# Expert selection by sorted maxima, the step's turnings reordered, and first semaphores raised earlier, in a one-core block of two layers

## What is computed

```python
def _hier_moe(h, w_rg, b_rg, w_re, b_re, w_g, w_u, w_d):
    ...
    g_prob = jax.nn.softmax((hf @ w_rg).astype(jnp.float32) + b_rg.astype(jnp.float32), axis=-1)
    g_top, g_idx = lax.top_k(g_prob, 1)
    e_logits = ((hf @ w_re).astype(jnp.float32) + b_re.astype(jnp.float32)).reshape(T, N_GROUPS, EXPERTS_PER_GROUP)
    e_in = jnp.take_along_axis(e_logits, g_idx[:, :, None], axis=1)[:, 0]
    e_top, e_idx = lax.top_k(jax.nn.softmax(e_in, axis=-1), TOP_K)
    wts = g_top * e_top / jnp.sum(e_top, axis=-1, keepdims=True)
    eid = g_idx * EXPERTS_PER_GROUP + e_idx
    ...
    def expert(args):
        xb, e = args
        return (jax.nn.silu(xb @ w_g[e]) * (xb @ w_u[e])) @ w_d[e]
```

## Time and profile before

| what | value |
|---|---|
| median of 3 runs | 701.5 us |
| lowest and highest | 700.43 and 703.64 us |
| the profiled execution | 699.65 us, its span 697.9 us |
| TensorE busy | 644.7 us, 92% |
| VectorE busy | 369.2 us, 53% |
| ScalarE busy | 283.5 us, 41% |
| mean granted clock of TensorE | 0.989 of full speed |
| moved by the transfers | 174.75 MB, mean 250 GB/s |

### The profile page before, as it was taken

One profiled execution on the slowest core, in us unless ns is written; L12 is line 12 of the kernel. 1 busy time (PEld: TensorE's weight loads), 2 busy tenths in 40 slices (PEclk: granted clock), 3 DMA queues, 4 the chain that ended last, 5 costly groups with the idle time before them and its releaser, 6 DMA issues.

```text
span 697.9 us, 11071 instructions
## 1 busy us (share of the span) xinstructions
PE 644.7 (92%) x4357; PEld 482.5 (69%) x4357; DVE 369.2 (53%) x651; ACT 283.5 (41%) x447; POOL 53.9 (8%) x74
## 2 busy tenths in 40 slices
PE   7999999899999999998999999799999986778793
PEld 4999997799999999995797888534444432224363
DVE  6686964777666777675686573621212120103275
ACT  6864463565555555545847621201101100010376
POOL 1000000400000000003185500000000000000000
PEclk9999999999999999999999999999999999899998
DMA  9944541657755555107604169999699999999901
GB/s 326 345 133 159 203 150 46 243 178 239 234 181 180 180 180 180 61 0 256 241 22 171 51 226 428 423 395 434 239 429 430 425 428 426 428 423 428 398 34 60
DMA packets 54488, 174.75 MB, mean 250 GB/s; under 512 B 4662, under 2 KB 29362, under 8 KB 48050
## 3 DMA queue, kind: packets, MB, share of 16 engines
q1 hardware_dynamic: 53776, 172.54, 64.4%
q10 hardware_dynamic: 674, 1.69, 0.6%
HBM read 173.17 MB, written 1.05 MB: 250 GB/s over the span
## 4 chain that ended last, share of the span: by engine, by line
PE 69%; DMA 13%; DVE 10%; ACT 5%; issue 2%; SPq 0%; POOL 0%; DVEq 0%; ACTq 0%; POOLq 0%
PE ps L1742 14%; PE ps L1743 14%; PE ps L1744 14%; DMA arena<-in_w_moe_dram 7%; PE ps L2249 6%; DMA W<-in_w_ple_gate_dram 6%; PE ps L2235 3%; PE ps L2259 3%; PE ps L2284 3%; PE ps L1939 2%; DVE wpg_low L1666 1%; PE ps L2087 1%; DVE arena L1413 1%; PE ps L1714 1%; PE ps L2038 1%
## 5 line engine op out<-in xcount | busy, mean ns | idle before, releaser
L1742 PE MATMUL ps<-hT_high,w_up_high 128*128 128x256 f32 x352 | 99.7, 283 | 1.7 <-DVE w_up_low L1249 1.7
L1744 PE MATMUL ps<-hT_high,w_up_low 128*128 128x256 f32 x352 | 99.6, 283 | 0.0
L1743 PE MATMUL ps<-hT_low,w_up_high 128*128 128x256 f32 x352 | 99.6, 283 | 0.0
L1742 PEld LDWEIGHTS ps<-hT_high,w_up_high 128*128 128x128 f32 x352 | 67.5, 192 | 2.6 <-DVE w_up_low L1249 2.2
L1743 PEld LDWEIGHTS ps<-hT_low,w_up_high 128*128 128x128 f32 x352 | 67.5, 192 | 0.3
L1744 PEld LDWEIGHTS ps<-hT_high,w_up_low 128*128 128x128 f32 x352 | 67.5, 192 | 0.0
L1249 DVE TENSOR_TENSOR w_up_low<-W,w_up_high 128x1024 fp32r<-128x1024 f32 x44 | 53.3, 1239 | 23.9 <-ACT w_up_high L783 23.9
L783 ACT CAST w_up_high<-W 128x1024 fp32r<-128x1024 f32 x44 | 44.6, 1047 | 28.5 <-PE ps L1744 28.5
L942 ACT ACTIVATE arena<-ps 128x256 f32<-128x256 f32 x9 | 3.4, 383 | 117.9 <-PE ps L2249 117.9
L1742 PE MATMUL ps<-h_high,dense_high 128*128 128x256 f32 x160 | 45.7, 286 | 0.0
L1743 PE MATMUL ps<-h_low,dense_high 128*128 128x256 f32 x160 | 45.3, 283 | 0.0
(11 more groups left out here) (471 smaller groups left out, 1364.1 us busy)
## 6 DMA issues: line engine op xcount, KB each, us to landing
W<-in_w_moe_dram SPq DMA_DIRECT2D x25, 2048.0 KB, 19.9
arena<-in_w_moe_dram SPq DMA_DIRECT2D x19, 2048.0 KB, 25.5
W<-in_w_up_dram SPq DMA_DIRECT2D x22, 1024.0 KB, 8.4
W<-in_w_in_dram SPq DMA_DIRECT2D x8, 2048.0 KB, 10.9
W<-in_w_down_dram SPq DMA_DIRECT2D x11, 1024.0 KB, 5.0
hh<-in_w_moe_dram SPq DMA_DIRECT2D x4, 2048.0 KB, 28.7
W<-in_w_out_dram SPq DMA_DIRECT2D x2, 2048.0 KB, 9.0
W<-in_w_o_dram SPq DMA_DIRECT2D x2, 2048.0 KB, 8.4
```

The costliest lines, as they stand in the source:

```text
L1742: pe.matmul(o, lhs[0], rhs[0], start=first, stop=False, skip_group_check=True)
L1743: pe.matmul(o, lhs[0], rhs[1], start=False, stop=False, skip_group_check=True)
L1744: return pe.matmul(o, lhs[1], rhs[0], start=False, stop=last_k, skip_group_check=True)
```

## The change

Five edits, all between the logits and the end of the expert loop:

- The best two experts come from a sorted list: `max` gives the eight largest of a token's 32 masked logits, `max_index` their places, for each token block by itself; a cast and two compares with the column numbers make the two masks. The mask of the other groups is made and applied in one instruction. For the groups the search stays as it was.
- The number of rounds is counted against eight marks, the first of them -1, instead of seven and an added one. The marks are written ahead of the last logits.
- VectorE raises its six first semaphores ahead of the scaling of the logits. TensorE raises its six between 4 and 10 zero products instead of behind its wait for the rounds, and the 19 zero products become 14.
- TensorE scatters one token block at a time and turns the activations between the two; the turning of the one-hots stays behind the second.
- ScalarE copies the activations ahead of the scatter weights.

```diff
@@ -309,11 +309,14 @@
         e32 = [v3(take(64), 2) for _ in range(3)]
         chosen = v3(take(32).bitcast(BF16), 2)
         ranks = e32[0]
-        off[0] += 80
+        top8, at8 = v3(take(16), 2), v3(take(16).bitcast(mybir.dt.uint32), 2)
+        atf = v3(take(4), 2)
+        off[0] += 28
         g4 = [v3(take(8), 2) for _ in range(4)]
         sm = [take(2) for _ in range(12)]
         rcnt = take(8)
-        rgt = take(56)
+        rgt = take(64)
+        marks = take(8)
@@ -940,10 +943,10 @@
 
                 act.wait_ge(sig("upw_used"), n * UPC + 2 * UPC)
                 act.activation(sg, ps[:, 2, 0:F_EXP], ACT.Silu).then_inc(sig("sg_ready"), 1)
+                act.wait_ge(sig("at_done"), n + 2)
+                act.copy(aT, v3(ps[:, 3, 0:256], 2)).then_inc(sig("aT_ready"), 1)
                 act.wait_ge(sig("oht_done"), n + 2)
                 act.copy(SC, ps[:, 0, 0:256]).then_inc(sig("sc_ready"), 1)
-                act.wait_ge(sig("at_done"), n + 2)
-                act.copy(aT, v3(ps[:, 3, 0:256], 2)).then_inc(sig("aT_ready"), 1)
@@ -1543,6 +1546,10 @@
                 dve.tensor_tensor(x_tok[:, b, :], x_tok[:, b, :],
                                   ps[:, 4 + 2 * b:6 + 2 * b, :].rearrange("p a b -> p (a b)"), ALU.add).then_inc(sig("x_ready"), 1)
                 turned(3, "norm_ffn_g_2", (2 * b, 2 * b + 1))
+            for name in ("hot_ready", "oh_ready", "ohw_ready", "xga_ready", "xgb_ready", "a_ready"):
+                dve.sem_inc(sig(name), 1)
+            link(dve.tensor_copy(marks, iot[:, 0:SEQ].rearrange("p (m t) -> p m t", t=CAP)[:, :, 0]))
+            link(dve.tensor_scalar(marks[:, 0:1], ones[:, 0:1], -1.0, None, ALU.mult))
             for b in range(TB):
                 dve.wait_ge(sig("std_ready"), 2 * 3 + b + 1)
                 link(dve.reciprocal(stat[:, 14 + b:15 + b], stat[:, 14 + b:15 + b]))
@@ -1555,42 +1562,41 @@
...
-            def first_max(vals, top, hot, io, n):
-
-                link(dve.tensor_reduce(top, vals, AX, ALU.max))
-                link(dve.tensor_tensor(hot, vals, wide(top, n), ALU.is_equal))
-                link(dve.scalar_tensor_tensor(hot, hot, -64.0, io, ALU.mult, ALU.add))
-                link(dve.tensor_reduce(sm[11], hot, AX, ALU.min))
-                link(dve.tensor_tensor(hot, hot, wide(sm[11], n), ALU.is_equal))
-
-            first_max(gl_, sm[0], g4[0], io4, N_GRP)
+            link(dve.tensor_reduce(sm[0], gl_, AX, ALU.max))
+            link(dve.tensor_tensor(g4[0], gl_, wide(sm[0], N_GRP), ALU.is_equal))
+            link(dve.scalar_tensor_tensor(g4[0], g4[0], -64.0, io4, ALU.mult, ALU.add))
+            link(dve.tensor_reduce(sm[11], g4[0], AX, ALU.min))
+            link(dve.tensor_tensor(g4[2], g4[0], wide(sm[11], N_GRP), ALU.not_equal))
             dve.tensor_tensor(g4[1], gl_, wide(sm[0], N_GRP), ALU.subtract).then_inc(sig("gsub_ready"), 1)
 
-            link(dve.tensor_scalar(g4[2], g4[0], -NEG, NEG, ALU.mult, ALU.add))
             em = e32[0]
-            link(dve.tensor_tensor(em.rearrange("p b (g e) -> p b g e", g=N_GRP),
-                                   el_.rearrange("p b (g e) -> p b g e", g=N_GRP),
-                                   g4[2].unsqueeze(3).broadcast_to([P, 2, N_GRP, EPG]), ALU.add))
-            first_max(em, sm[1], e32[1], io32, N_EXP)
-            link(dve.scalar_tensor_tensor(em, e32[1], 3 * NEG, em, ALU.mult, ALU.add))
-            first_max(em, sm[2], e32[2], io32, N_EXP)
+            link(dve.scalar_tensor_tensor(em.rearrange("p b (g e) -> p b g e", g=N_GRP),
+                                          g4[2].unsqueeze(3).broadcast_to([P, 2, N_GRP, EPG]), NEG,
+                                          el_.rearrange("p b (g e) -> p b g e", g=N_GRP), ALU.mult, ALU.add))
+            for b in range(TB):
+                dve.max(top8[:, b, :], em[:, b, :]).then_inc(sig("top_ready"), 1)
+            for b in range(TB):
+                dve.wait_ge(sig("top_ready"), b + 1)
+                dve.max_index(at8[:, b, :], top8[:, b, :], em[:, b, :]).then_inc(sig("top_found"), 1)
+            dve.wait_ge(sig("top_found"), 2)
+            link(dve.tensor_copy(atf, at8[:, :, 0:2]))
+            for i in range(2):
+                dve.tensor_tensor(e32[1 + i], io32, atf[:, :, i:i + 1].broadcast_to([P, 2, N_EXP]), ALU.is_equal)\
+                   .then_inc(sig("top_marked"), 1)
+            dve.wait_ge(sig("top_marked"), 2)
             dve.tensor_tensor(chosen, e32[1], e32[2], ALU.add).then_inc(sig("sel_ready"), 1)
-            dve.tensor_tensor(sm[4], sm[2], sm[1], ALU.subtract).then_inc(sig("msub_ready"), 1)
+            dve.tensor_tensor(sm[4].unsqueeze(2), top8[:, :, 1:2], top8[:, :, 0:1], ALU.subtract).then_inc(sig("msub_ready"), 1)
             dve.wait_ge(sig("rank_done"), at("rank_done", 1))
             dve.wait_ge(sig("sel_ready"), at("sel_ready", 1))
...
-            marks = iot[:, 0:SEQ].rearrange("p (m t) -> p m t", t=CAP)[:, 1:MAXR, 0]
-            link(dve.tensor_tensor(v3(rgt, 8), rcnt.unsqueeze(2).broadcast_to([P, NGRP8, MAXR - 1]),
-                                   marks.unsqueeze(1).broadcast_to([P, NGRP8, MAXR - 1]), ALU.is_gt))
+            link(dve.tensor_tensor(v3(rgt, 8), rcnt.unsqueeze(2).broadcast_to([P, NGRP8, MAXR]),
+                                   marks.unsqueeze(1).broadcast_to([P, NGRP8, MAXR]), ALU.is_gt))
             link(dve.tensor_reduce(rtab[:, 0:8], v3(rgt, 8), AX, ALU.add))
-            link(dve.tensor_scalar(rtab[:, 0:8], rtab[:, 0:8], 1.0, None, ALU.add))
             link(dve.tensor_tensor_scan(rtab[:, 8:16], ones[:, 0:8], rtab[:, 0:8], 0.0, ALU.mult, ALU.add))
             dve.tensor_copy(rint, rtab).then_inc(sig("rounds_ready"), 1)
             link(dve.scalar_tensor_tensor(ranks, v3(ps[:, 3, 0:64], 2), 1.0, chosen, ALU.add, ALU.mult))
             link(dve.tensor_scalar(RK, ranks, -1.0, None, ALU.add))
-            for name in ("hot_ready", "oh_ready", "ohw_ready", "xga_ready", "xgb_ready", "a_ready"):
-                dve.sem_inc(sig(name), 1)
@@ -2203,7 +2209,10 @@
             turn_x(3, 1)
             logits(1)
             tri, every = counts[:, 0:P], counts[:, P:2 * P]
-            keep_busy(2, 19)
+            keep_busy(2, 4)
+            for name, n in (("gxa_done", 1), ("gxb_done", 1), ("oht_done", 1), ("at_done", 1), ("upw_used", UPC), ("downw_used", DNC)):
+                pe.sem_inc(sig(name), n)
+            keep_busy(2, 10)
             pe.wait_ge(sig("sel_ready"), at("sel_ready", 1))
             pe.matmul(ps[:, 3, 0:32], tri, chosen[:, 0, :], start=True, stop=True)
@@ -2218,8 +2227,6 @@
             keep_busy(2, 3)
             pe.wait_ge(sig("rounds_ready"), 1)
             pe.wait_ge(sig("step_clear"), 2)
-            for name, n in (("gxa_done", 1), ("gxb_done", 1), ("oht_done", 1), ("at_done", 1), ("upw_used", UPC), ("downw_used", DNC)):
-                pe.sem_inc(sig(name), n)
...
-            def scatter(n, signal="scatter_done"):
+            def scatter(n, b, signal="scatter_done"):
 
                 pe.wait_ge(sig("ypa_ready"), n + 1)
                 pe.wait_ge(sig("ypb_ready"), n + 1)
-                for b in range(TB):
-                    for half in range(2):
-                        last = pe.matmul(ps[:, 4 + 2 * b + half, :], SC[:, b * P:(b + 1) * P], Yp[:, half, :],
-                                         start=False, stop=True, skip_group_check=True)
-                    last.then_inc(sig(signal), 1)
+                for half in range(2):
+                    last = pe.matmul(ps[:, 4 + 2 * b + half, :], SC[:, b * P:(b + 1) * P], Yp[:, half, :],
+                                     start=False, stop=True, skip_group_check=True)
+                last.then_inc(sig(signal), 1)
@@ -2289,9 +2295,10 @@
             def pe_step(n, g):
                 gather(n, g)
                 expert_up(n, g)
-                scatter(n)
+                scatter(n, 0)
+                turn_act(n)
+                scatter(n, 1)
                 turn(n)
-                turn_act(n)
                 expert_down(n, g)
@@ -2318,7 +2325,8 @@
                 with pe.Fori(0, rounds) as r:
                     pe_step(begun + r, g)
                 begun = pe.value_load(rint[0:1, 8 + g:9 + g], min_val=1, max_val=NGRP8 * MAXR)
-            scatter(begun, "moe_done")
+            for b in range(TB):
+                scatter(begun, b, "moe_done")
```

## The result

| | before | after |
|---|---|---|
| median of 8 runs each | 702.21 us | 698.03 us |
| lowest and highest | 700.43 and 703.64 us | 695.75 and 700.55 us |
| ratio, with 95% interval | | 0.9941 (0.9926 to 0.9955) |
| the profiled execution, its span | 699.65, 697.9 us | 695.75, 694.0 us |
| mean granted clock | 0.989 | 0.980 |

The change made the kernel 4.2 us, 0.59%, faster (3.2 to 5.2 us by the interval). That is just beyond the 0.5% that a measurement of this kernel can tell. The span of the profiled execution is 3.9 us shorter.

A forecast was written before the change was run, and what follows sets the result against it. Bound by TensorE until the transfers' stop near 491 to 496 us, by weight transfers behind it. Start of the gather 2.4 us plus two steps 1.0 us made 3.4 us, off 701.5: 698.1 us, range 696.5 to 701.0.

The forecast's parts named there:

- count of rounds: On VectorE, counting the rounds loses one linked addition: 0.21 us saved.
- load behind the hole: SyncE's weight load issued at 495.47 us, ending the transfers' stop in the expert stage: claimed 3.4 us sooner.
- The limit: From the load behind the hole on, transfers set the time: the end moves as much as that load, later savings are lost.
- The choice: Choosing experts on VectorE: 14 instructions of 3.51 us become a sorted choice of 1.90 us, saving 1.61 us.
- The slow rival: In the choice on VectorE, new operations cost a scan's 8 ns an element: 1.0 us later, time 699.1 us, chance 0.12.
- The raises: Between rounds and first gather, VectorE's six raises cost 0.60 us, all saved; TensorE's own preparation lay hidden beside VectorE.
- the first case of my two: VectorE's moved raises run while the last product is in the pipe, so the 0.99 us wait for TensorE hides them.
- The bubble: TensorE's raises among the zero products might make the ranks wait 0.2 us; counted as nothing.
- The step: From scatter to first down product, 0.96 us becomes 0.46: 0.50 us saved a step, 1.0 us for two steps.
- The cap: The load behind the hole can come about 6 us sooner before the transfers themselves are the limit.
- The hole left: The transfers' stop in the expert stage was to shorten to about 2.6 us.
- The slower rival, the clock: TensorE's clock falls on the gate products: 7 us at 1.2 GHz cost 3.5 us, 10.5 us give 703.4 us; chance 0.08.

The follow-up runs named there:

- delay_behind: Kernel after with 12 more zero products in each step of groups 2 to 7; ratio to before 0.9937 (0.9916 to 0.9957), 698.23 us.
- delay_ahead: Kernel after with 12 more zero products in each step of groups 0 and 1; ratio to before 1.001 (0.999 to 1.003), 703.05 us.
- sel_only: Kernel before with the sorted choice of experts alone, 19 zero products kept; ratio to before 0.9976 (0.9954 to 0.9997).
- zero19: Kernel after with 4 and 15 zero products instead of 4 and 10; not timed, in its trace the rank products start 3.82 us behind the choice's start instead of 3.19.
- dve_raises: Kernel before with only VectorE's six raises moved ahead; not timed, in its trace the gather starts 2.21 us behind the rounds, as before.
- pe_raises: Kernel before with only TensorE's six raises moved, between 4 and 15 zero products; not timed, in its trace the gather starts 2.20 us behind the rounds.
- skip_if: Kernel after with TensorE jumping over the scatter in the first round of group 0; 696.67 us, ratio to before 0.9914 (0.9894 to 0.9934).
- step_only: Kernel before with the scatter in two parts, activations turned between them and copied first, alone; ratio to before 0.9987 (0.9967 to 1.0006).
- sem_only: Kernel before with both engines' raises moved, TensorE's between 4 and 15 zero products; ratio to before 0.9976 (0.9964 to 0.9988).
- after_again: Kernel after, unchanged, run once more beside skip_if; 697.68 us, ratio to before 0.9934 (0.9916 to 0.9953).

## Why the prediction was right

The forecast was 698.1 us, the median is 698.03. That they agree to 0.1 us is luck: two misses cancel. The forecast took 3.4 us off the median of three runs, 701.5; the median of all eight is 702.21, 0.7 us more, and the change brought 4.2 us, 0.8 more than forecast. Right were the limit and the way from each part to the end; every term was a little small. By steps:

| step | predicted, us | measured, us |
|---|---|---|
| choice, to the end of the sum | 1.61 | 1.74 |
| count of rounds | 0.21 | 0.24 |
| raises, rounds to gather | 0.60 | 0.69 |
| start of the gather | 2.4 | 2.67 |
| two steps | 1.0 | 1.17 |
| load behind the hole | 3.4 | 3.84 |
| landing of the gate weights, on the clock of the trace | 3.4 | 3.93 |

**The limit.** The transfers behind the hole kept their length (121.41 and 120.98 us to the gate load's issue), the stretch behind the last landing too (38.29 us), and what was saved there came to nothing. delay_behind and delay_ahead show both halves.

**The choice.** I took MAX as one pass of 0.192 us started 0.12 us ahead of the next, and that was right: 0.185 us each, and two in 0.29 us. I took MAX_INDEX as two passes of 0.19 us started 0.12 us apart; it is a load of the eight values of 0.07 to 0.09 us, and a search of 0.18 that starts 0.06 to 0.08 us behind the load. Here lie the 0.13 us that the term was small: the second search ended 0.90 us behind the start of the masked addition, where I had 1.03. The slow rival, the scan's price of 8 ns an element, is wrong: 32 elements cost 0.185 us in all. It was one scan of the trace, 4x256 in 2.05 us; two others of the kernel before take 0.68 us for 4x256 and 1.22 us for 128x512, under 3 ns an element, and would have made the rival 0.3 us instead of 1.0. The Trainium skill's "Vector Engine (DVE) Microarchitecture Reference", section 3.9, has the positions found by two instructions; the trace agrees, MATCH_VALUE_LOAD and FIND_INDEX8 stand there as two rows each time. The 1.74 us could all be had only because five zero products went: sel_only and zero19 put that at 0.7 and 0.6 us.

**The raises.** The sum was right within 0.1 us, its reason half wrong. I had booked VectorE's 0.60 us as the path and TensorE's preparation as hidden beside it, "still hidden, barely". That holds without the raises on either side. But in the kernel before, TensorE's six raises, which I priced at VectorE's 0.10 us, cost at least 0.12 to 0.13 each behind its wait for the rounds, and TensorE was as late as VectorE (2.21 us behind the rounds in dve_raises, 2.20 for VectorE in pe_raises). I had named VectorE alone as the path; dve_raises, which moves VectorE's alone, gains nothing at all. A pair of equally late engines looks in the chain of waits like one of them, since the chain names only the last.

VectorE's raises hid where I had put them, the first case of my two: from the turning of the second token block to the next instruction VectorE takes 1.20 us with the six raises between (440.38 to 441.58 us after) and without (440.08 to 441.28 before).

The bubble that I had counted at nothing was nothing: 4.27 us for 19 zero products with and without raises among them. The Trainium skill's "TensorE: Matmul & The Clock Gate", in the section on the array's architectural detail, gives TensorE a queue of 64 instructions, and by that the raises run ahead of the products still queued; the rows agree with it, though no run here varies the depth.

**The step.** Mis-sized by 0.08 us a step. I had 0.50 of the 0.96 us between scatter and down products, it became 0.52; beyond that the down products themselves went from 3.64 to 3.57 us. They start behind a wait for ScalarE before, and no longer do; in skip_if's first step, where they do again, they take 3.64.

**The cap.** "The issue can come about 6 us sooner" was too low, and the reason is a step that failed. I had taken the hole's start, near 489.7 us, as fixed by bytes already under way. By the shares, added up, the transfers stopped near 489.66 us before and 488.78 after, 46.74 and 45.57 us behind the start of the choice: 1.17 us sooner. Two stretches, 456 to 460 us, first of the kernel before, then of after:

```profile
456.00:460.00 4.00, 4.00 (x44) 1.25 (x40) 1.04 (x3) 0.00 (x0) 0.00 (x0) 1.00 0.89 348
```

```profile
456.00:460.00 4.00, 4.00 (x40) 1.04 (x32) 0.00 (x0) 0.00 (x0) 0.00 (x0) 1.00 0.99 422
```

Before, the transfers had a dent here. The first slots of the expert stage came free, and the next load was issued, at 457.48 us before and 455.10 after, and with the earlier issue the dent is gone. That the transfers ran short of work there is a reading, and the other traces bear it out: in step_only, dve_raises and pe_raises the same load is issued 14.5 to 14.6 us behind the start of the choice, as before (14.56), and of the two whole microseconds behind it the lower has 246, 311 and 279 GB/s (197 before); in sel_only and sem_only it is issued at 13.5 and 13.8 us, and the lower has 410 in both. So the cap, counted on the gate load, is about 173.96 - 166.28 = 7.7 us, of which the change takes 4.3. It did not bind here.

**The hole left.** I expected it 3.4 us shorter, 2.6 us long. By the shares that are left unused it went from 6.7 us (489 to 500 us before) to 4.0, 2.7 less. It is the same step: the hole's end moved by 3.84, its start by 1.17 us.

**The slower rival, the clock.** I had put it on the gate products, behind TensorE's idleness from 622 us on, with 0.08. The gate products kept 1.00. But the mechanism is there, one stage earlier and smaller: the last down products, and in two of the three the last scatter, partly or wholly at 1.2 GHz, which costs 1.4 to 2.4 us, in three of eight executions. I had written that idleness in the other seven steps is given back for nothing. In the last of them it is not quite nothing. Three of the eight runs of the kernel after lie at 699.97 to 700.55 us and the other five at 695.75 to 698.08; the fall would fit them, but they have no traces, and the profiled execution of after_again (699.38 us) had another reason, a choice that started 3.4 us later. What makes that start vary was not tried.

**The chances.** I had 0.55 on "within 0.5%" and 0.40 on faster, because the 3.4 us summed to 0.48%. The terms were all a little small, by 0.44 us together, and that put the median on the other side of the line, at 0.59%; the interval, 0.45 to 0.74%, holds the line.

## What to carry to other kernels

Find the last place where the transfers stop: a microsecond in front of it counts in full, behind it nothing, except that the last step before the end still showed (1.1 us in delay_behind), and that the clock of an engine that waits there may fall (1.4 to 2.4 us in three of eight executions). Where a wait in the chain names one engine, ask how late the second one is before counting a gain: here two moves were worth nothing apart and 0.7 us together. When something ahead of filler work gets faster, cut the filler by as much, or it becomes the wait.
